# A fifteenth gate pair by the seven-product scheme, and two token blocks made earlier

## What is computed

```python
    y_d = forgetting_attention(d_q, d_k, d_v, d_f, fox_b_f) * jax.nn.silu(d_z)
    ys = jnp.stack([y_a, y_b, y_c, y_d], axis=0)
    branch_d = jnp.einsum('nbsw,nwd->bsnd', ys, w_branch)
    g = jax.nn.sigmoid(gates.reshape(bsz, s, N_BRANCH, d))
    merged = jnp.sum(g * branch_d, axis=2)
    return x + merged @ w_out
```

## Time and profile before

| | us |
|---|---|
| median of 3 runs (1106.61 to 1106.88) | 1106.66 |
| the profiled execution | 1106.82 |
| its span, first to last instruction | 1104.9 |
| TensorE busy in the span | 1096.4 (99%) |
| VectorE busy | 748.9 (68%) |
| ScalarE busy | 517.5 (47%) |
| granted TensorE clock, mean | 0.998 of full speed |

### The profile page before, as it was taken

The page is one execution under the profiler, slowest core; times in us unless marked ns, Lnnn a source line. Parts: engine busy times, 40 slices in busy tenths (PEclk is TensorE's granted clock), DMA queues, the critical chain, the costliest instruction groups (busy, mean ns, idle before and its releaser), DMA issues.

```text
span 1104.9 us, 17994 instructions
## 1 busy us (share of the span) xinstructions
PE 1096.4 (99%) x7298; PEld 928.7 (84%) x7298; DVE 748.9 (68%) x1202; ACT 517.5 (47%) x870; POOL 17.8 (2%) x40
## 2 busy tenths in 40 slices
PE   9999999999999999999999999999999999999997
PEld 8888888888888888878888887887789999999986
DVE  6876876954676247458789887447568777667853
ACT  7662354324675235544453535336544444444543
POOL 1000000000001001000000000000000000000000
PEclk9999999999999999999999999999999999999999
DMA  9543324422214422622222232231121322333241
GB/s 371 221 152 125 120 74 133 125 98 78 77 58 144 161 90 104 200 66 86 79 77 96 77 96 77 63 109 58 58 77 58 115 100 73 115 114 115 83 185 77
DMA packets 33618, 121.09 MB, mean 110 GB/s; under 512 B 3824, under 2 KB 3824, under 8 KB 33536
## 3 DMA queue, kind: packets, MB, share of 16 engines
q1 hardware_dynamic: 30672, 109.88, 29.2%
q0 software_dynamic: 2720, 10.03, 2.6%
q10 hardware_dynamic: 144, 0.03, 0.0%
HBM read 115.74 MB, written 4.19 MB: 109 GB/s over the span
## 4 chain that ended last, share of the span: by engine, by line
PE 98%; DMA 1%; ACT 0%; SPq 0%; DVE 0%; issue 0%
PE acc L1896 22%; PE acc L1898 22%; PE acc L1897 22%; PE acc L1908 2%; PE side L1908 2%; PE acc L1906 2%; PE side L1906 2%; PE acc L1904 2%; PE side L1904 2%; PE side L1896 2%; PE side L1897 2%; PE side L1898 2%; PE acc L2271 2%; PE side L2051 2%; PE side L2271 1%; PE side L2123 1%
## 5 line engine op out<-in xcount | busy, mean ns | idle before, releaser
L1201 DVE TENSOR_TENSOR w_lo<-raw,w_hi 128x1024 fp32r<-128x1024 f32 (+2 forms) x194 | 225.7, 1165 | 148.9 <-ACT w_hi L665 146.1
L1896 PE MATMUL acc<-hT_hi,w_hi 128*128 128x512 f32 x648 | 258.6, 399 | 0.0
L1898 PE MATMUL acc<-hT_hi,w_lo 128*128 128x512 f32 x648 | 252.8, 390 | 0.0
L1897 PE MATMUL acc<-hT_lo,w_hi 128*128 128x512 f32 x648 | 252.4, 389 | 0.0
L665 ACT ACTIVATE w_hi<-raw 128x1024 fp32r<-128x1024 f32 (+2 forms) x194 | 195.4, 1008 | 109.8 <-PE acc L1898 82.4
L1896 PEld LDWEIGHTS acc<-hT_hi,w_hi 128*128 128x128 f32 x648 | 121.8, 188 | 27.1 <-issue 2.4
L1898 PEld LDWEIGHTS acc<-hT_hi,w_lo 128*128 128x128 f32 x648 | 121.6, 188 | 26.0
L1897 PEld LDWEIGHTS acc<-hT_lo,w_hi 128*128 128x128 f32 x648 | 121.9, 188 | 23.6
L1896 PE MATMUL acc<-w_hi,hT_hi 128*128 128x512 f32 (+1 forms) x152 | 59.9, 394 | 0.0
L1898 PE MATMUL acc<-w_hi,hT_lo 128*128 128x512 f32 (+1 forms) x152 | 58.8, 387 | 0.0
L1897 PE MATMUL acc<-w_lo,hT_hi 128*128 128x512 f32 (+1 forms) x152 | 58.7, 386 | 0.0
(11 more groups left out here) (482 smaller groups left out, 2249.0 us busy)
## 6 DMA issues: line engine op xcount, KB each, us to landing
raw<-in_ga SPq DMA_DIRECT2D x32, 512.0 KB, 4.8
ada_raw<-in_ada SPq DMA_DIRECT2D x16, 512.0 KB, 11.5
raw<-in_wo SPq DMA_DIRECT2D x16, 512.0 KB, 3.5
raw<-in_br SPq DMA_DIRECT2D x16, 512.0 KB, 3.5
raw<-in_q SPq DMA_DIRECT2D x8, 512.0 KB, 3.5
raw<-in_u SPq DMA_DIRECT2D x8, 512.0 KB, 3.9
raw<-in_gp SPq DMA_DIRECT2D x8, 512.0 KB, 4.8
raw<-in_ada_w SPq DMA_DIRECT2D x8, 512.0 KB, 3.5
```

The source lines that it names most:

```text
L1201: nc.vector.tensor_tensor(out=lo[:, 0:width], in0=strip_of(k), in1=hi[:, 0:width].bitcast(f32), op=ALU.subtract).then_inc(lo_made, 1)
L1896: nc.tensor.matmul(ps, w[0], x[0], start=first, stop=False)
L1897: nc.tensor.matmul(ps, w[0], x[1], start=False, stop=False)
L1898: return nc.tensor.matmul(ps, w[1], x[0], start=False, stop=last)
```

## The change

`FIRST_PAIR` goes from 2 to 1: panels `ga` 2 and 3, two plain units, become the units `sa`, `sb`, `sc`, `sd` of pair 1, and `br` 1 is computed among them. 30 of 32 panels then go by the scheme. What pair 1 needs moves ahead: `t3` in full is computed at `dz` 3 in place of `ga` 1, `t4` at `ga` 0 in place of `ga` 2, the `t4` upper part at `ga` 0, `t3` into `hT_hi` at `ga` 1 (with a new wait for `ga` 1's matmuls) and into `hT_lo` at `br` 0. The finishing steps of branch d go from `ga` 0 to `ga` 1. The first pair's weight sums have a buffer of their own, and which of `acc` and `side` a pair uses is swapped.

```diff
-FIRST_PAIR, LAST_PAIR = 2, 2 * KT - 1
+FIRST_PAIR, LAST_PAIR = 1, 2 * KT - 1
@@
-D_FINAL_AT = SLOT0 + max(t for t, l in SUM_AT.items() if l) + 1
+D_FINAL_AT = SLOT0 + max(t for t, l in SUM_AT.items() if l) + 2
@@
-        t3_part = at("t3_part", M + 24576, [P, 4, HALF])
-        t3_full = at("t3_full", M + 28672, [P, 4, HALF])
+        s12_first = at("s12_first", M + 4096, [P, 2, 4 * P])
+        t3_part = at("t3_part", M + 8192, [P, 4, HALF])
+        t3_full = at("t3_full", M + 12288, [P, 4, HALF])
@@
-        def banks_of(p):
-            return side if p % 2 == 0 else acc
+        def banks_of(j):
+            return side if (j - FIRST_PAIR) % 2 == 0 else acc
@@ ScalarE
-                if (kind, j) == ("ga", 3):
+                if (kind, j) == ("ga", 0):
                     act.wait_ge(t_step, T_STEP[4, "full"])
                     nc.scalar.activation(t_hi[4][:, :, :], t_full[4][:, :, :], ACT.Copy).then_inc(t_hi_made, 1)
+                if (kind, j) == ("ga", 1):
+                    act.wait_ge(unit_used, STEP["ga", 1] + 1)
                     act.wait_ge(t_step, T_STEP[3, "full"])
                     nc.scalar.activation(quarter(hT_hi, 0, 1), t3_full[:, :, :], ACT.Copy).then_inc(t_hi_made, 1)
@@ VectorE
-                if (kind, j) == ("ga", 1):
+                if (kind, j) == ("dz", 3):
                     difference(t3_full[:, :, :], t3_part[:, :, :], hi[1, 1], lo[1, 1], hi[0, 1], lo[0, 1])
-                if (kind, j) == ("ga", 2):
+                if (kind, j) == ("ga", 0):
+                    dve.wait_ge(exp_made, 2 * SPARSE)
+                    dve.wait_ge(summed, sums_done(2 * SPARSE - 1))
                     dve.wait_ge(t_step, T_STEP[2, "lo"])
                     difference(full[4], rest[4], hi[1, 0], lo[1, 0],
                                t_hi[2][:, :, :].bitcast(f32), t_lo[2][:, :, :].bitcast(f32))
-                if (kind, j) == ("ga", 3):
+                if (kind, j) == ("ga", 1):
...
-                if (kind, j) == ("br", 1):
+                if (kind, j) == ("br", 0):
                     dve.wait_ge(t_step, T_STEP[3, "full"])
                     dve.wait_ge(t_hi_made, 4)
@@ TensorE, unit br of a pair
+                        if p == 0:
+                            pe.wait_ge(y_made, 1 + FINAL.index((name, 3)))
```

More of the change, by code:

```diff
@@ L518, in strip_of, with s12_of @@
             return raw[:, UNIT[kind, j] % RING, 0:WIDTH.get(kind, U)]
-        def banks_of(p):
-            return side if p % 2 == 0 else acc
+        def s12_of(j):
+            return s12_first if j == FIRST_PAIR else s12
+        def banks_of(j):
+            return side if (j - FIRST_PAIR) % 2 == 0 else acc
         def ada_tile(j):
@@ L1208, in combine @@
                     return
+                part = s12_of(j)
                 a, b, n = raw_of(("ga", 2 * j)), raw_of(("ga", 2 * j + 1)), j - FIRST_PAIR + 1
@@ L1212, in combine @@
                         dve.wait_ge(raw_in[UNIT[u] % RING], 16 * (UNIT[u] // RING + 1))
-                    then(nc.vector.tensor_tensor(out=s12[:, 0, :], in0=b[:, 0:512], in1=b[:, 512:1024], op=ALU.add))
-                    nc.vector.tensor_tensor(out=s12[:, 1, :], in0=s12[:, 0, :], in1=a[:, 0:512], op=ALU.subtract)\
+                    then(nc.vector.tensor_tensor(out=part[:, 0, :], in0=b[:, 0:512], in1=b[:, 512:1024], op=ALU.add))
+                    nc.vector.tensor_tensor(out=part[:, 1, :], in0=part[:, 0, :], in1=a[:, 0:512], op=ALU.subtract)\
                         .then_inc(combined, 1)
@@ L1221, in combine @@
                     dve.wait_ge(lo_made, STEP["sa", j] + 1)
-                    nc.vector.tensor_tensor(out=a[:, 512:1024], in0=a[:, 512:1024], in1=s12[:, 1, :], op=ALU.subtract)\
+                    nc.vector.tensor_tensor(out=a[:, 512:1024], in0=a[:, 512:1024], in1=part[:, 1, :], op=ALU.subtract)\
                         .then_inc(combined, 1)
@@ L1288, in gate_pair @@
                         first = j % 2 == 0 and o == 1
-                        nc.vector.tensor_tensor(out=total if first else merged_part[:, :], in0=(acc if o == 0 else side)[3][:, :],
+                        nc.vector.tensor_tensor(out=total if first else merged_part[:, :], in0=(side if o == 0 else acc)[3][:, :],
                                                 in1=sig[:, o, :], op=ALU.mult).then_inc(gated, 1)
@@ L1854, in _ @@
                         wait_tile(dve, (kind, j), t)
-                        nc.vector.tensor_tensor(out=x2[t][:, 0:S], in0=side[t][:, :], in1=x2[t][:, 0:S],
+                        nc.vector.tensor_tensor(out=x2[t][:, 0:S], in0=acc[t][:, :], in1=x2[t][:, 0:S],
                                                 op=ALU.add).then_inc(freed["dve"], 1)
@@ L1875, in _ @@
                         wait_tile(dve, (kind, j), t)
-                        nc.vector.tensor_tensor(out=x2[t][:, S:D], in0=acc[t][:, :], in1=x2[t][:, S:D],
+                        nc.vector.tensor_tensor(out=x2[t][:, S:D], in0=side[t][:, :], in1=x2[t][:, S:D],
                                                 op=ALU.add).then_inc(freed["dve"], 1)
@@ L1938, in strassen @@
                     if p == 0:
-                        wait_freed(pe, RESULT["br", 1] + 1)
+                        wait_freed(pe, RESULT["br", 0] + 1)
                     else:
@@ L1949, in strassen @@
                         name = "abcd"[2 * (j % 2) + o]
+                        if p == 0:
+                            pe.wait_ge(y_made, 1 + FINAL.index((name, 3)))
                         for kt in range(4):
                             cols = slice((4 * o + kt) * P, (4 * o + kt + 1) * P)
-                            ins = product((acc if o == 0 else side)[3][:, :], (hi[:, cols], lo[:, cols]),
+                            ins = product((side if o == 0 else acc)[3][:, :], (hi[:, cols], lo[:, cols]),
                                           (y_hi[name][:, kt, :], y_lo[name][:, kt, :]), kt == 0, kt == 3)
@@ L1998, in token_units @@
                                 pe.wait_ge(gated, 2 * (LAST_PAIR - FIRST_PAIR + 1))
-                            ps = (side if j - i < per else acc)[t]
+                            ps = (acc if j - i < per else side)[t]
                         else:
```

4 lines of the change are left out of this document (2 added, 2 removed).

## The result

| | median of the runs | lowest to highest | profiled execution, its span | mean granted clock |
|---|---|---|---|---|
| before, 6 runs | 1106.78 us | 1106.61 to 1106.88 | 1106.82, 1104.9 us | |
| after, 6 runs | 1112.45 us | 1111.77 to 1113.05 | 1112.42, 1110.5 us | 0.996 |

The ratio is 1.0051, 95% interval 1.004 to 1.0063: 5.67 us slower; forecast were +5.2 us and 1111.9, with a range from 1109.5 to 1113.4. Note the scatter too: the runs before lie within 0.27 us, those after over 1.28 us.

What follows compares the result with a forecast made beforehand. TensorE, busy for 1096.4 of 1104.9 us, was taken as the bound. Tile gain -0.77, wait +4.4 and low clock +1.6 gave +5.2 us on 1106.82, 1112.0; as a median 1111.9, range 1109.5 to 1113.4.

Steps and rivals of the forecast that it cites:

- The scheme tile: On TensorE, one output tile changes from plain, 16.32 us, to the scheme, 15.55 us: 0.77 us gained.
- The walk of both engines: VectorE and ScalarE operations followed in changed order from 804.2 us, to find when TensorE's `gate_a` copy is ready: 829.8.
- The wait: TensorE in the middle of `sb` 1 wants the `gate_a` copy at 825.35, has it at 829.8: 4.4 us lost.
- Its cause: Finishing steps, then sigmoid, `t3` into `hT_hi` and two `w_hi` stand ahead of the `gate_a` copy in ScalarE's queue.
- rival 3: The `gate_a` copy comes in time, TensorE never waits in `sb` 1, only the gain is left: 1105.9; chance 0.05.
- The second wait: In `br` 1, before the product reading VectorE's `w_lo` of `sc` 1: 0.7 us, vanishing if the clock is low.
- The lowered clock: TensorE's clock falls during the 4.4 us wait and runs slow afterwards: 1.6 us lost, bounds 0 and 1.9.
- Rival 1: The clock holds through the wait in `sb` 1: +4.3 us, 1111.0; chance 0.30.
- Rival 2: The wait in `sb` 1 is shorter, at half 2.2 us, clock holds: 1108.1 to 1109.1; chance 0.12.
- Rival 4: Late `br` 2 or VectorE's backlog disturbs pairs 2 and 3: 1 to 2 us more, 1113.0 to 1114.0; chance 0.08.
- What costs nothing: Pair 1's seven extra small VectorE operations, bank copies, `acc`/`side` swap and later `br` 2 load: no cost.

Runs made afterwards that it cites:

- interleaved: Changed kernel, finishing steps back at `ga` 0, `t4` operations and `w_lo` of `sb` 1 in their idle gaps, ScalarE's splits and copies reordered: 1106.34 us.
- copy_first: Changed kernel with ScalarE's first `gate_a` copy of pair 1 moved ahead of `w_hi` of `sc` 1: 1111.26 us.
- filled_wait: Changed kernel with 18 extra, unread matmuls of 512 columns in `sb` 1 before the wait for the `gate_a` copy: 1111.33 us.
- half_filled_wait: Changed kernel with 9 extra, unread matmuls of 512 columns in `sb` 1 before the wait for the `gate_a` copy: 1111.51 us.
- finals_back: Changed kernel with the four finishing steps of branch d back one unit earlier, at `ga` 0, ahead of the `t4` block: 1112.51 us.
- products_in_place: Changed kernel with branch d's finishing products written into their own `z_d` tiles, the next product made before the last subtraction: 1107.89 us.
- gaps_filled_only: Changed kernel, finishing steps back at `ga` 0, `t4`'s three operations in their gaps, its upper part behind `gate_a`, lower part behind `w_lo` of `sc` 1: 1108.28 us.
- moves_without_scheme: Kernel before, pair 1 still plain, with the moves of `t3`, `t4` and the finishing steps alone, the two `t3` stores left in place: 1107.11 us.
- after_again: The changed kernel, unedited, run again in another group: 1112.83 us.
- t4_behind: Changed kernel with the `t4` block one unit later, at `ga` 1, behind the four finishing steps: 1112.99 us.

## Why the prediction was right, and which term was off

- **The scheme tile saves 0.77 us.** Right. In interleaved, in which no wait is left, the tile takes 15.55 us for 16.32; its time is 0.71 us under before, which the interval does not prove.
- **The walk of both engines.** `t4` was to end at 814.8 and the first `y_tmp` to start at 818.0; measured 814.3 and 817.57, in an execution 0.20 us earlier. The copy was to be there at 829.8; it was at 829.37. The wait is 4.27 us for 4.4.
- **Its cause.** ScalarE's queue holds the copy back, as said. What the prediction didn't say is that the copy could be freed and little would be won: rival 3 names ScalarE's queue as the one mechanism, and copy_first, which takes 1.2 us of it away, is still 4.2 us slower, with the floor where it was. No kernel here has that copy fully in time over the unshortened row; that it would still wait for the floor is worked out from the row's length, which did not move. The second wait, set down as a small follower of 0.7 us, is the real floor. Measured where the first is covered (filled_wait), it is 834.57 - 829.75 - 4.16 = 0.66 us, so its size was right and its rank was not.
- **The lowered clock: the term that was mis-sized.** The step "Since the fall comes late in the wait I take 1.6", with bounds of 0 and 1.9, measured 2.34 us, over the upper bound. The bound came from the program's start, where 3.8 us ran slow; here the clock stayed low for 4.9 us after TensorE went on. Taken against the floor, which would have cost 0.66 us of it anyway, the fall costs 1.68 net (32.37 - 30.69) where the forecast had 1.6 - 0.7 = 0.9. That the clock falls in the wait, and holds back what follows, was right; how long it stays low no row of before could tell, and why it differs here was not shown. The 0.74 us that the term was short, less the 0.13 by which the wait was shorter, are the 0.6 us by which 1112.45 lies over 1111.9.
- **Rival 1, the clock holds, 1111.0.** Not what happened, but well sized: filled_wait, copy_first and the traced run of half_filled_wait are this case, at +4.2 to +4.4. The traced run of finals_back comes to the same (+4.16), though the clock fell in it, for it was back before the floor.
- **Rival 2, a wait half as long.** products_in_place and gaps_filled_only show what would have made it: work in the idle gaps of the finishing chain. That the clock holds through 2.2 us of waiting, as the rival assumes, is not sure: in finals_back it fell in an idle time of 2.45 us.
- **Rival 4, a disturbance further on.** It did not come. There is no second gap up to 1106 us, so the late load of `br` 2 cost nothing.
- **What costs nothing.** The moves tried in moves_without_scheme: 1107.11 against 1107.10.

## What to carry to other kernels

Where a bottleneck engine starts to wait, don't stop at the instruction that releases it: follow the in-order row of the engine behind, to the last thing that is needed from it, and compare that row's length with the work beside it. Reordering inside such a row moves the wait; making it shorter removes it. Here that was done by filling its idle gaps (four of 0.77 us and one of 2.08) and by putting one operation of 1.1 us, which is needed only later, behind its end; the two were not tried apart, but products_in_place, which leaves that operation in its place, is 3.3 us shorter by closing most of the four gaps. A wait on TensorE has a second price: in the changed kernel 4.27 us of it cost another 2.34 us at the lowered clock, 1.68 net of the floor, and with waits of 2.0 to 2.5 us of idle time it fell in some executions. A scatter of the runs that the other kernel doesn't have is the sign to look for it.

## What the runs showed of the hardware

The fall of the granted clock has no fixed delay behind the last matmul. In the changed kernel it came after 2.2 us of idle, in finals_back after 2.2 (the slice from 826 to 827 reads 0.66, so it was full for 0.32 us of it; the last matmul ended at 824.12), in after_again after 2.3 (0.96 from 827 to 828; 825.58), in t4_behind after 2.7 (0.87 from 828 to 829; 826.02), in copy_first not within 2.86 us. Nor has its return: the low stretch lasted 6.8 us in the changed kernel (827.5 to 834.3), in after_again (827.9 to 834.8) and in t4_behind (828.7 to 835.6), 3.4 us in finals_back (826.3 to 829.7), TensorE being at work in the latter part of each. finals_back:

```profile
826.00:827.00 1.00, 0.43 (x2) 0.66 0.00 0
827.00:828.00 1.00, 1.00 (x6) 0.50 0.00 0
828.00:829.00 1.00, 1.00 (x7) 0.50 0.00 0
829.00:830.00 1.00, 0.83 (x5) 0.63 0.00 0
```

So the time of one program can depend on when the clock falls and comes back: the runs of finals_back are at 1111.2 to 1111.3 or at 1112.5 to 1112.9. The scatter of the other runs fits their mean clocks, but only one execution of each kernel has a trace, so that it has this cause in each of them was not shown.
